# The seven-product form in gate, up and down of both middle blocks, its weight sums on GpSimd there and in the last stage

## The reference

```python
# middle block (twice): D_MODEL = 1024, FFN_DIM = 2816
x = x + merged @ w_o
u = causal_dwconv(rms_norm(x, norm2_g) @ w_up, ffn_conv_w) + ffn_conv_b   # 3 taps, 5632 columns
u_gate, u_val = jnp.split(u, 2, axis=-1)
return x + (jax.nn.silu(u_gate) * u_val) @ w_down

# last block
h2 = rmsnorm_3(x, norm2_w[l])
f = (jax.nn.silu(h2 @ w_ffn_gate[l]) * (h2 @ w_ffn_up[l])) @ w_ffn_down[l]
```

## Time and profile before

| | |
|---|---|
| runs, median (lowest to highest) | 2145.76 us (2143.68 to 2146.35), 3 runs |
| the profiled execution | 2145.23 us, its span 2143.5 us |
| TensorE's granted clock, mean | 0.995 of full speed |
| TensorE busy | 2119.8 us (99%) |
| VectorE busy | 906.1 us (42%) |
| ScalarE busy | 381.4 us (18%) |
| GpSimd busy | 33.3 us (2%) |
| gate and up of L0, iterations | 746.4 to 884.6 us of the span |
| down of L0 | 884.6 to 960.9 us |
| the last stage's gate and up | 1935.9 to 2064.7 us |

### The profile page before, as it was taken

How to read it: one execution, slowest core, us unless ns; L and a number is a source line. 1 busy time by engine, 2 the same in 40 slices (tenths; PEclk the granted TensorE clock), 3 DMA queues, 4 the chain that set the end, 5 groups by cost and what they waited for, 6 DMA issues and landing times.

```text
span 2143.5 us, 29709 instructions
## 1 busy us (share of the span) xinstructions
PE 2119.8 (99%) x10538; PEld 1832.4 (85%) x10538; DVE 906.1 (42%) x2393; ACT 381.4 (18%) x944; POOL 33.3 (2%) x52
## 2 busy tenths in 40 slices
PE   8999999999999999999999999999999999999998
PEld 6658788888888888888888888888888888889998
DVE  4133434963342255301991453155501023318772
ACT  2231421112111111100121112111101114311000
POOL 0000010000000000000000000000000000000000
PEclk9999999999999999999999999999999999999999
DMA  5304434434343444444443343444444432344543
GB/s 202 117 20 136 136 135 146 140 118 137 124 140 129 151 146 154 152 157 142 143 139 132 122 138 118 153 142 157 156 143 152 137 137 99 108 150 159 175 168 128
DMA packets 42269, 296.81 MB, mean 138 GB/s; under 512 B 4800, under 2 KB 4928, under 8 KB 8512
## 3 DMA queue, kind: packets, MB, share of 16 engines
q1 hardware_dynamic: 42176, 295.55, 40.3%
HBM read 294.48 MB, written 1.05 MB: 138 GB/s over the span
## 4 chain that ended last, share of the span: by engine, by line
PE 97%; DVE 1%; DMA 1%; ACT 0%; issue 0%; SPq 0%; ACTq 0%; DVEq 0%
PE bank L647 96%; DMA ring<-wstream 1%; PE bank L646 1%; DVE arena L1454 0%; DVE arena L1778 0%; DVE arena L1771 0%; ACT arena L1101 0%; DVE tmp L1774 0%; ACT arena L1205 0%; DVE xn L1471 0%; DVE tmp L1459 0%; ACT arena L1157 0%; DVE arena L1699 0%; DVE arena L1691 0%; DVE arena L2115 0%
## 5 line engine op out<-in xcount | busy, mean ns | idle before, releaser
L647 PE MATMUL bank<-xn,ring 128*128 128x256 f32 (+2 forms) x4896 | 1037.3, 373 | 0.5 <-DMA ring<-wstream 0.5
L647 PEld LDWEIGHTS bank<-xn,ring 128*128 128x128 f32 x4896 | 904.2, 190 | 127.9 <-issue 3.7
L647 PE MATMUL bank<-arena,ring 128*128 128x256 f32 (+3 forms) x3462 | 734.8, 372 | 12.6 <-DMA ring<-wstream 10.7
L647 PEld LDWEIGHTS bank<-arena,ring 128*128 128x128 f32 x3462 | 632.0, 191 | 106.6 <-DMA ring<-wstream 12.1
L1101 ACT ACTIVATE arena<-bank 128x256 f32 (+5 forms) x360 | 142.0, 398 | 971.9 <-PE bank L647 850.5
L1454 DVE SCALAR_TENSOR_TENSOR arena<-arena,par (+2 forms) x712 | 299.8, 480 | 24.5 <-DVE arena L2010 3.2
L647 PE MATMUL bank<-arena 128*128 128x128 f32 (+9 forms) x832 | 141.7, 318 | 2.8 <-DVE arena L2119 1.9
L647 PEld LDWEIGHTS bank<-arena 128*128 128x128 f32 (+5 forms) x832 | 108.2, 189 | 27.6 <-issue 17.9
L1454 DVE SCALAR_TENSOR_TENSOR x_res<-bank,x_res 128x256 f32<-128x256 f32 x42 | 17.8, 425 | 224.2 <-PE bank L647 224.2
L1454 DVE SCALAR_TENSOR_TENSOR arena<-arena,bank 128x256 f32<-128x256 f32 (+3 forms) x60 | 24.4, 423 | 138.8 <-ACT arena L1101 122.9
L1124 ACT ACTIVATE arena<-x_res,par 128x256 f32<-128x256 f32 x40 | 20.3, 508 | 296.4 <-DVE x_res L1454 296.4
(11 more groups left out here) (196 smaller groups left out, 980.1 us busy)
## 6 DMA issues: line engine op xcount, KB each, us to landing
ring<-wstream SPq DMA_DIRECT2D x262, 1024.0 KB, 4.8
ring<-wstream SPq DMA_DIRECT2D x15, 768.0 KB, 4.2
cst<-consts SPq DMA_DIRECT2D x1, 2616.0 KB, 15.2
ring<-wstream SPq DMA_DIRECT2D x4, 512.0 KB, 3.8
h_res<-tokens SPq DMA_DIRECT2D x2, 544.0 KB, 5.5
out<-arena SPq DMA_DIRECT2D x1, 1024.0 KB, 4.0
ring<-wstream SPq DMA_DIRECT2D x2, 384.0 KB, 3.1
ring<-wstream SPq DMA_DIRECT2D x2, 288.0 KB, 2.7
```

The source lines that it names most:

```text
L647: return pe.matmul(o, lhs, rhs, start=start, stop=stop, skip_group_check=True)
```

## The change

The feed-forward iterations of both middle blocks take the seven-product form, and the sums of weights move to GpSimd there and in the last stage.

- The weight stream of L0.up, L1.up, L0.down and L1.down is laid out in quarters like C's. Down becomes four groups of three blocks. The ten iterations of gate and up are written out and no longer a loop.
- `mix` stands in GpSimd's program, behind the `gather` of the norm ahead: all blocks of L0, then L1's gathers, and so on. It waits for the slot to land and for TensorE's last product of the block before in the same slot, whose sums it overwrites.
- `fast_block` waits for the sums in three steps (`mix1`, `mix2`, `mixed`), and frees its slot after the "x" products; SyncE's load now waits for that and for the slot's `mixed` too.
- In the middle blocks `unite` writes into `ffp`, ahead of which two columns of zeros stand for the convolution. The first tap, with the bias, moves from VectorE to ScalarE (`tap`, an Identity with scale and bias from SBUF). The other two stay on VectorE, as do SiLU's product and the product of gate and up, now one operation of 512 columns each instead of two of 256.
- `sum_acts` runs in the middle blocks too: once after the norm, and for down after iterations 7, 9 and 10.
- The residual of the middle blocks' down is one operation of 512 columns for two tiles (`fast_residual`), and the following `boundary` on ScalarE waits for pairs of tiles.

```diff
@@ stream_plan @@
-        pl(n + "up", "w_up_2", l, 10, 2, 8, two(256, FFN + 256))
-        add(n + "down", "w_down_2", l, its=2, n=6, size=None, part=down_part)
+        add(n + "up", "w_up_2", l, its=10, n=2, size=2048,
+            part=lambda w, it, q: quarters(w, FFN * q + 256 * it + 256, range(4), 4))
+        add(n + "down", "w_down_2", l, its=4, n=3, size=None, part=down_quarters)
@@ sync: load @@
                     sp.wait_ge(sems[f"slot_done{slot}"], n)
+                    if held[slot]:
+                        sp.wait_ge(*e.at(("mixed", held[slot])))
+                    held[slot] = (*stage.split("."), i, q) if stage in FAST else None
@@ tensor: fast_block @@
                 product("x", 1, w[:, 2], lambda k: acts_of(sums, 3, k)).then_inc(
-                    *e.done("main_done", ("pe", (key, "x")) if last else None))
+                    *e.done(f"slot_done{slot}", ("pe", (key, "x")) if last else None))
                 claim("y")
-                pe.wait_ge(*e.at(("mixed", block)))
-                product("y", 1, m[:, 0], lambda k: acts_of(sums, 0, k), opens=True).then_inc(*e.done(f"slot_done{slot}"))
+                pe.wait_ge(*e.at(("mix1", block)))
+                product("y", 1, m[:, 0], lambda k: acts_of(sums, 0, k), opens=True)
                 pe.wait_ge(*e.at((sums, "sum", 2)))
                 product("y", 2, m[:, 1], lambda k: acts_of(sums, 2, k))
+                pe.wait_ge(*e.at(("mix2", block)))
                 product("y", 3, m[:, 2], lambda k: acts_of(sums, 1, k))
+                pe.wait_ge(*e.at(("mixed", block)))
@@ tensor, middle blocks @@
-                blocks(L + "up", 8, x256, S, ready=normed(L + "n2"))
-                down_product(L + "down", lambda k: hf[:, k, :], S, [(L + "hf",)])
+                fast_ffn(f"L{l}", hf, 4)
@@ scalar, middle blocks, for it in range(10), for q in range(2) @@
+                        first_product((F, "up", it, q), q)
+                        for part in ("c11", "c12", "c22"):
+                            act.wait_ge(*e.at(((F, "up", it, q), part)))
...
+                            act.activation(fo[:, 2 * q + t, :], ffp[:, 2 * q + t, 0:S], ACT.Identity,
+                                           scale=G(f"ffn_conv_w_2.{l}", 3 * j),
+                                           bias=G(f"ffn_conv_b_2.{l}", j)).then_inc(*e.step((F, "tap", it, q, t)))
@@ gpsimd @@
-            for key in ("L0.n2", "L1.n1", "L1.n2", "C.n1", "C.n2"):
-                gather(key, S, sq)
+            def mix(block):
...
+                pool.wait_ge(sems[f"landed{slot}"], 16 * turn)
+                if before_in_slot(block):
+                    pool.wait_ge(*e.at(("pe", (before_in_slot(block), "t"))))
+                pool.tensor_tensor(out=m[:, 0:2 * size], in0=w[:, size:3 * size], in1=w[:, 0:2 * size],
+                                   op=ALU.subtract).then_inc(*e.step(("mix1", block)))
+                pool.wait_ge(*e.at(("mix1", block)))
+                pool.tensor_tensor(out=m[:, 2 * size:3 * size], in0=m[:, size:2 * size], in1=w[:, 0:size],
+                                   op=ALU.add).then_inc(*e.step(("mix2", block)))
+                pool.wait_ge(*e.at(("mix2", block)))
+                pool.tensor_tensor(out=m[:, 3 * size:4 * size], in0=w[:, 3 * size:4 * size],
+                                   in1=m[:, 2 * size:3 * size], op=ALU.subtract).then_inc(*e.step(("mixed", block)))
+            for L in ("L0", "L1", "C"):
+                if L != "L0":
+                    gather(L + ".n1", S, sq)
+                gather(L + ".n2", S, sq)
+                for b in fast_blocks:
+                    if b[0] == L:
+                        mix(b)
@@ vector, middle blocks, for it in range(10) @@
+                    for q in range(2):
+                        unite((F, "up", it, q), q, ffp[:, 2 * q:2 * q + 2, :], 2,
...
+                        for k in (1, 2):
+                            for t in range(2):
...
+                                stt(fo[:, 2 * q + t, :], ffp[:, 2 * q + t, k:k + S], G(g("ffn_conv_w_2"), 3 * j + k),
+                                    fo[:, 2 * q + t, :], ALU.mult, ALU.add).then_inc(
+                                    *e.step((F, "half" if k == 1 else "conv", it, q, t)))
+                    dve.wait_ge(*e.at((F, "ft", it)))
+                    stt(flat(fo[:, 0:2, :]), flat(ft), 1.0, flat(fo[:, 0:2, :]), ALU.add, ALU.mult).then_inc(*e.step((F, "fo", it)))
...
+                    dve.tensor_tensor(hf[:, 2 * it + 2:2 * it + 4, :], fo[:, 0:2, :], fo[:, 2:4, :],
+                                      ALU.mult).then_inc(*e.step((F, "hf", it + 1)))
+                    hidden_sums(F, it, hf, sum_down_l)
+                fast_residual(F, 4, both_l)
```

More of the change, by code:

```diff
@@ L600, in _ @@
             at_col, n_block = 0, 0
+            held = [None, None]
             def load(stage, i):
@@ L695, in out_product, with fast_block @@
                     halves(stage, q, 8, [P, P], rhs, T, ready=None if q else ready)
[L697 to L709 removed]
+            def fast_block(block, key, plain, sums, first=True, last=True, held=None, ready=None):
+                slot, n = e.next_block(), pairs_of(block)
                 w = ring[:, slot, 0:4 * n * P].rearrange("p (s k c) -> p s k c", s=4, c=P)
[L711 removed]
+                m = mixed_of(block).rearrange("p (s k c) -> p s k c", s=4, c=P)
                 banks = held or {}
@@ new lines, in hidden_sums, with fast_residual @@
+            def hidden_sums(L, it, hidden, dst):
+                for r, ks in enumerate(DOWN_PAIRS):
+                    if it + 1 == (7, 9, 10)[r]:
+                        dve.wait_ge(*e.at((L, "hf", it + 1)))
+                        sum_acts((L, "down", r), hidden, dst[:, :, ks[0]:ks[-1] + 1])
+            def fast_residual(L, pairs, both):
+                for it in range(pairs):
+                    unite((L, "down", it), it, both, 0, (L, "x", it - 1) if it else (L, "hf", 10))
+                    stt(x_res[:, 2 * it:2 * it + 2, :], both, 0.5, x_res[:, 2 * it:2 * it + 2, :], ALU.mult,
+                        ALU.add).then_inc(*e.step((L, "x", it)))
@@ L1984, in _ @@
                 normed(L + "n2", xg_f)
+                for j in range(ND):
+                    dve.wait_ge(*e.at((L + "n2", "xn", j)))
+                sum_acts((f"L{l}", "up"), xn[:, :, 0:S], sum_up_l)
                 for t in range(2):
@@ L2024, in _ @@
+                    hidden_sums(F, it, hf, sum_down_l)
+                fast_residual(F, 4, both_l)
+                for it in range(4):
+                    dve.wait_ge(*e.at((F, "x", it)))
             invert("C.n1")
```

247 lines of the change are left out of this document (111 added, 136 removed).

## The result

The change takes 2207.48 us (median of 4 runs, 2206.33 to 2208.59), the kernel before 2146.06 beside it (4 runs, 2143.68 to 2147.59): a ratio of 1.029, 95% interval 1.0269 to 1.0305, or 61 us slower. The forecast of 2190 lay 17 under it and had sign and mechanism right.

The account below looks back on a forecast made before the run. TensorE, busy 99%, was taken to bound the kernel; without collision 41.3 us came off 2145.2. With VectorE and GpSimd taking turns, +42.4 for both middle blocks and +1.9 for the last stage made +44.3: 2190, range 2110 to 2238.

Parts of the forecast that it names:

- 2148, the lower end: Whole kernel: low end of the forecast's own range, with iterations of 14.4, a start of 4 and no sums.
- +42 a block: Each middle block: loss with iterations of 17.8 and both extras in full, giving about 2235 for the whole.
- The bound and the gain with nothing in the way: Whole kernel: TensorE bounds it; without collisions 41.3 us come off, to 2104.
- GpSimd's price, 5.2 a block: Weight sums on GpSimd: 2.41 + 1.28 + 1.28 and waits make 5.2 us, under TensorE's 6.25 a block.
- Exposed and free operations: VectorE, gate and up iteration: 5.2 us with both inputs in SBUF collide; 5.0 of bank inputs or waits don't.
- An iteration of 15.6 (14.4 to 19.4): Middle blocks' gate and up: VectorE's 10.2 plus 5.4 of GpSimd's sums make 15.6 us, against TensorE's 12.5.
- hidden sums: Middle blocks, after iterations 7 and 9: eight VectorE activation sums of 0.69, exposed, adding 5 us (0 to 8).
- The start, 8 us: Middle block's start: normalising beside sums costs 3.8, activation sums and first taps about 4 more; 8 (4 to 8).
- The last stage, +1.9: Last stage: only its start loses, 3.8 for collision less 1.9 for sums no longer waited for on VectorE.
- No collision: Rival: nothing collides, blocking being a matter of scalar-column operations alone; 2104, faster; chance 0.16.
- Finer sharing: Rival: the port is shared finer than whole instructions, or turns fall out well; 2104 to 2148; chance 0.10.
- GpSimd at 6.0 a block: Rival: GpSimd's sums take 6.0 us a block, iterations 17.2, the whole 2227; chance 0.06.

Follow-up runs that it names:

- e1: The change with each of GpSimd's three sums cut to 8 columns, all waits kept, so TensorE multiplies stale columns: 2106.1 us, ratio 0.982.
- e6: The change with the middle blocks' taps, SiLU's product and product of gate and up taking one input from a bank: 2152.9 us, ratio 1.0028.
- e9: The change with each of GpSimd's sums cut into pieces of 256 columns, same results: 2161.9 us, ratio 1.0071.
- e8: The change with the last stage's sums of weights back on VectorE, in three steps: 2202.8 us, ratio 1.0264.
- e10: e7 with the last stage's sums of weights back on VectorE: 2116.9 us, ratio 0.986.
- e2: The change with each of GpSimd's sums replaced by a constant fill of the same columns, reading nothing: 2107.8 us, ratio 0.9825.
- e3: The change with gate and up of the middle blocks back in the plain form, down kept: 2140.1 us, ratio 0.9976.
- e5: The change with gate alone in the seven-product form in the middle blocks' iterations, up plain: 2142.5 us, ratio 0.9985.
- e7: e6 with the norm's inverse copied to a bank and the first two tiles' taps in banks too: 2121.6 us, ratio 0.988.
- e11: e10 with GpSimd's 1024-column sum cut in two of 512: 2114.1 us, ratio 0.9851.

## Why the prediction was right, and where it was short

The mechanism is the one forecast; the sum fell short. The profiled execution lost 63.4 us for 44.3: 7.9 more than forecast in L0, 4.0 in L1, 4.3 in the last stage and 3.3 in the mixers, less 0.5 ahead of the first norm. Two slips of the sum itself: 2148, the lower end, leaves out the last stage's 1.9, and +42 a block should be +44 by its own terms (188.7 - 138.2 - 6.5), which is what 2235 was added up with. The tap's price was read from a group that isn't the feed-forward's: the 480 operations of the earlier trace rows with 478 ns run in the mixers; the feed-forward's own took 484, so little changes.

**The bound and the gain with nothing in the way: right.** 2104 was worked out, and e1 measures 2106.1, 3.3 of it the longer mixers. 6.25 us a block, 125.0 for gate and up and no other price stand in its rows. Down was to take 68.8 and takes 70.3, 1.5 of it the slow clock of its first block (4.35 us for 24 products that take 2.84). The boundary behind down costs 1.8 (6.89 us from down's end to the next norm's row before, 8.69 after) for 1.0. Of this 0.5 is the last residual, which takes 1.23 us for 0.69 beside GpSimd's additions for the next norm; the prediction had put these at nothing.

**GpSimd's price, 5.2 a block: right.** Its sums that meet no operation of VectorE take 2.36 and 1.27 us; those that do are longer, 2.48 and 1.40 in the mean.

**Exposed and free operations: right.** Unites keep 0.28 and 0.42, what has both inputs in SBUF doesn't; e6 shows it by moving one input to a bank.

**An iteration of 15.6 (14.4 to 19.4): right in size, the stage's sum partly by luck.** The starts of tanh (L1358) in L0 stand at 778.86 and 922.96, nine intervals of 144.1 us in all. Four are 15.7 to 15.9, three 12.7 to 13.7, and two, with hidden sums, 20.4 and 21.5. The sum had 9 x 15.6 + 5 = 145.4. The seven plain ones have a mean of 14.6 and come to 7 us less than forecast, the two others to 5.6 more (41.8 for 36.2): the eight hidden sums take 14.4 us of VectorE's time, where 5 stood. Its reasoning, the port's time added up, only happens to fit: e9 falls to 13.4 with more port time. What e9 points to is how long one instruction can stand in the other's way.

**The start, 8 us: the step that failed.** It is larger than the whole miss in L0's gate and up. The wait before the first block is 3.38 in L0 (3.8 forecast), but before the third 9.61, where "about 4 more" stood. I had let one block's sums meet the norm, and one more the activation sums and the first taps. The timeline shows four blocks' sums in that time, against 30 operations of VectorE that end 16.9 late, and the first unite stands behind all of them. That TensorE waits 13.0 and not 16.9 is, as I read it, what two free blocks and the slow clock in them cover. Waits of 13.0, and 3.3 of slow clock behind them, make 16.3 for 8. The remaining 30.0 of the 46.3 lost in that stretch compare with 32.9 forecast for iterations and hidden sums. The stage comes to 171.3 for 165.9. L1 has 166.7: waits of 3.44, 1.23 and 3.52 at its start and 4.6 of slow clock behind them make 12.8 for 8, and the remaining 28.9 again compare with 32.9.

**The clock: a term that was missing.** Behind the 3.38 and the 9.70 the granted clock is 0.54 and 0.59 over the next 3.5 and 3.7 us, so mostly the lower of its two levels (1.2 of 2.4 GHz), and the first sixteen products cost 1.5 to 1.8 us more. In L0's gate and up this makes the 7.9. In the feed-forward parts of the change, e6, e8 and e9 there are seventeen waits of 4.28 to 9.73 us, and every one is followed by slow products; of those between 1.8 and 3.5 some are (2.93 in L1 of the change: 3.59 us for sixteen) and some not (3.07 there: 2.02). A row of before showed it, and I read over it: in the earlier trace rows the 24 products behind the 1.89 take 4.54 us for 2.84.

**The last stage, +1.9: mis-sized.** It is +6.2. The term for the sums waited for on VectorE was -1.9 and is -3.1 (e8 against before), the 1.7 of slow clock in that row with it; e8 gets it with the sums still on VectorE, by waiting for them in three steps. The term for the collision at the start was 3.8 and is 9.3 (the change against e8): waits of 3.42, 0.49 and 1.09 where e8 has one of 0.44, and 4.3 of slow clock, as the first block's products take 3.75, 2.07 and 4.36 us for 1.95, 1.06 and 2.84. Behind the start most iterations there do take 12.5, so 6.25 a block.

**The rivals.** No collision (0.16): refuted, taps at 0.81. Finer sharing (0.10): refuted, a blocked operation begins when the other's ends, and 2207 lies far above its 2148. GpSimd at 6.0 a block (0.06): refuted by 2.36 and 1.27.

**The mixers, 3.3 us.** Here too it is the clock, with TensorE busy throughout. A window of L1's mixer before, then the same place after, and one in C's mixer after:

```profile
1128.80:1135.60 6.80, 6.80 (x26) 5.68 (x25) 2.18 (x6) 0.84 (x3) 0.00 (x0) 0.75 0.00 0
...
1156.00:1162.80 6.80, 6.80 (x17) 4.95 (x16) 1.68 (x3) 0.00 (x0) 0.00 (x0) 0.50 0.12 52
...
1787.50:1790.90 3.40, 3.40 (x9) 2.69 (x9) 0.36 (x1) 0.00 (x0) 0.00 (x0) 0.50 0.05 19
```

In each case TensorE had just run a row of small products (`bank<-tmp,cst`, 16 to 32 of them). Before, half of the first window is at the lower level; after, all of it, and C's mixer has a slow stretch where before has none. Each of the two, 3.4 us more at half the clock, makes 1.7 us. The traces of all eleven other kernels fit: L1's mixer takes 435.5 us with the clock as before (e6, e8, e10) and 437.2 with it as after (the change, e1, e2, e3, e5, e7, e9, e11). The change isn't the cause as far as seen, since e6 and e8 have the same sums; what decides how long the clock stays low there stays open.

## What to carry to other kernels

Before work is moved to GpSimd beside VectorE, list which of VectorE's operations there have both inputs in SBUF; those pay, and with them everything behind them in its queue, so look above all at a stage's start, where TensorE has nothing in hand. The remedy is cheap where a bank is free: one input from PSUM brought the change from 2207 to 2122 us, and cutting GpSimd's longest instructions helped in both kernels where it was tried (2207 to 2162, and 2117 to 2114). Charge each long wait of TensorE (4.3 us and more in these traces) with another 1.5 to 3.0 us for the slow clock behind it. And before a step of a few us is explained by an edit, compare the granted clock in the sections that the edit doesn't touch.

## What the runs showed of the hardware

- A GpSimd fill of 1024 columns (0.95 us) doesn't hold off VectorE's operations with two SBUF tensors (seven start 0.35 us apart beside it, as without it), but holds one with a scalar column from 0.41 to 0.74 (e2).
- VectorE's operations with one input from a bank run at their own pace beside GpSimd's sums: taps 484 ns and products of gate and up 687 ns in e6, unites 0.28 and 0.42 in the change.
- The same sums cost the kernel 61 us in instructions of 1024 and 512 columns and 16 in instructions of 256 (e9).
- Behind TensorE's waits of 4.28 us and more sixteen products took 3.46 to 3.76 us for 1.95, and 24 took 4.35 to 5.16 for 2.84.
- The granted clock also fell with TensorE busy: in L1's mixer half or all of a stretch of 6.8 us was at the lower level, 435.5 or 437.2 us for the same instructions.
